# A 4 MB store of zero rows, issued behind the scan loop instead of ahead of it

## The reference

```python
h = rmsnorm(x) * (1 + sc1) + sh1
z = h @ w_in                                  # q | k | v | u
att = dilated_attn_prompt(q, k, v)            # or dilated_attn_decode with 2048 cached rows
ssm_y, hT_re, hT_im = s5_branch(u, h0, ...)   # scan over positions; last states are outputs
mixed = concat(rmsnorm(att), rmsnorm(ssm_y))
x = x + g1 * (mixed @ w_out)
h2 = rmsnorm(x) * (1 + sc2) + sh2
x = x + g2 * hier_moe(h2)                     # top 2 of 16 experts for each token
y = rmsnorm(x)
# outputs: y, new k and v, last scan states of the prompt (ssm_p) and of the samples (ssm_s)
```

## Time and profile before

| what | value |
|---|---|
| median of 3 runs | 1109.52 us (1108.87, 1109.52, 1143.79) |
| profiled execution, span from first to last instruction | 1138.1 us |
| mean granted TensorE clock in it | 0.855 |
| PE busy | 914.7 us (80%) |
| DVE busy | 378.3 us (33%) |
| POOL busy | 205.6 us (18%) |
| DMA moved | 231.09 MB, mean 203 GB/s |
| POOL's queue (q0) | 21.12 MB |
| the zero store | 4096 KB, issued at 369.99 us, landed 30.7 us later |

### The profile page before, as it was taken

The page is one execution under the profiler, slowest core; times in us unless marked ns, Lnnn a source line. Parts: engine busy times, 40 slices in busy tenths (PEclk is TensorE's granted clock), DMA queues, the critical chain, the costliest instruction groups (busy, mean ns, idle before and its releaser), DMA issues.

```text
span 1138.1 us, 11619 instructions
## 1 busy us (share of the span) xinstructions
PE 914.7 (80%) x4582; PEld 544.7 (48%) x4582; DVE 378.3 (33%) x790; ACT 162.5 (14%) x346; POOL 205.6 (18%) x311
## 2 busy tenths in 40 slices
PE   2525999999999665756769839999999999998920
PEld 2425884875666553543325434444444444444410
DVE  3021233112223989997126350111111111110118
ACT  1212000002224011011302100111111101111023
POOL 1234000014000466675100000000000000000043
PEclk9967999965569878778789758999999999999975
DMA  9969301160000936060343485498998999899252
GB/s 316 381 196 391 148 18 64 66 231 19 9 19 11 267 163 259 1 259 28 137 121 135 168 294 200 172 346 309 345 349 312 339 348 340 310 352 343 83 190 82
DMA packets 91428, 231.09 MB, mean 203 GB/s; under 512 B 3436, under 2 KB 12812, under 8 KB 89173
## 3 DMA queue, kind: packets, MB, share of 16 engines
q1 hardware_dynamic: 78630, 195.69, 47.8%
q0 software_dynamic: 5840, 21.12, 5.7%
q10 hardware_dynamic: 6912, 13.65, 3.2%
HBM read 213.37 MB, written 21.27 MB: 206 GB/s over the span
## 4 chain that ended last, share of the span: by engine, by line
PE 65%; DVE 14%; DMA 11%; issue 4%; SPq 4%; POOL 2%; ACT 1%; ACTq 0%; DVEq 0%; POOLq 0%
PE ps L1944 22%; PE ps L1963 11%; PE ps L1623 8%; DMA ring<-in_ada_w 5%; PE ps L1849 4%; PE ps L1532 4%; PE ps L1659 3%; PE ps L1657 3%; DMA out_ssm_s<-sample_states 3%; PE ps L1606 2%; PE ps L1675 2%; DVE s_xi L1169 2%; DMA ring<-in_w_in 2%; DVE s_gi L1182 2%; DVE s_gr L1180 2%
## 5 line engine op out<-in xcount | busy, mean ns | idle before, releaser
L1944 PE MATMUL ps<-ering,xgT 128*128 128x512 f32 x576 | 255.4, 597 | 5.0 <-ACT xgT L679 3.9
L1944 PEld LDWEIGHTS ps<-ering,xgT 128*128 128x128 f32 x576 | 108.8, 192 | 135.6 <-issue 133.3
L1963 PE MATMUL ps<-ering,aT 128*128 128x512 f32 x288 | 126.8, 593 | 3.1 <-ACT aT L679 3.1
L1623 PE MATMUL ps<-hT,ring 128*128 128x272 f32 x384 | 90.4, 399 | 1.9 <-DMA ring<-in_w_in 1.9
L1963 PEld LDWEIGHTS ps<-ering,aT 128*128 128x128 f32 x288 | 53.5, 190 | 64.8 <-issue 61.2
L1623 PEld LDWEIGHTS ps<-hT,ring 128*128 128x128 f32 x384 | 74.1, 193 | 17.9 <-issue 2.5
L645 POOL DMA_INDIRECT xg<-h_d,gidx x18 | 17.0, 943 | 338.8 <-PE ps L1532 305.0
L1849 PE MATMUL ps<-ring,mixT 128*128 128x512 f32 x128 | 63.5, 658 | 9.4 <-DVE pt L1314 9.1
L1543 PE MATMUL ps<-ring,silu_c 128*32 128x128 f32 x768 | 33.5, 347 | 43.3 <-DMA ring<-in_ada_w 42.6
L1453 DVE SCALAR_TENSOR_TENSOR a_s<-a_t,ps 128x512 f32<-128x512 f32 x18 | 12.4, 688 | 119.6 <-ACT a_t L679 119.6
L1543 PEld LDWEIGHTS ps<-ring,silu_c 128*32 128x32 f32 x768 | 29.6, 142 | 46.7 <-issue 32.5
(11 more groups left out here) (357 smaller groups left out, 1180.3 us busy)
## 6 DMA issues: line engine op xcount, KB each, us to landing
ering<-in_w_gate SPq DMA_DIRECT2D x18, 2048.0 KB, 14.6
ering<-in_w_up SPq DMA_DIRECT2D x18, 2048.0 KB, 20.2
ering<-in_w_down SPq DMA_DIRECT2D x18, 2048.0 KB, 9.8
ring<-in_ada_w SPq DMA_DIRECT2D x12, 2048.0 KB, 19.8
ring<-in_cache_k SPq DMA_DIRECT2D x8, 1792.0 KB, 9.9
ring<-in_cache_v SPq DMA_DIRECT2D x8, 1792.0 KB, 14.3
y_d<-ysb ACTq DMA_DIRECT2D x18, 512.0 KB, 8.2
ring<-in_w_in SPq DMA_DIRECT2D x4, 2048.0 KB, 18.3
```

What stands on the lines that cost most here:

```text
L1623: ins = mm(out, r[:, 512 * k + P * c:512 * k + P * (c + 1)], hT[:, k, cols], start=k == 0, stop=k == KD - 1)
L1944: ins = mm(ps[:, 2 * w + u, :], xgT[:, u, k, :], r[:, 512 * k:512 * (k + 1)], start=k == 0, stop=k == KD - 1)
L1963: ins = mm(ps[:, 6 + n, :], aT[:, u, c, :], r[:, D * c + 512 * n:D * c + 512 * (n + 1)], start=c == 0, stop=c == 3)
```

## The change

The line that issues the zero store is moved from its place ahead of the store of the samples' states to the place behind the 16 steps of the scan loop, ahead of the two stores of the prompt's last states. Nothing else is changed, in what is computed or in the waits.

```diff
         pool.dma_start(glu[:, 0, :, :], I["glu_a"]).then_inc(s("glul"), 16)
         pool.dma_start(glu[:, 1, :, :], I["glu_b"]).then_inc(s("glul"), 16)
 
-        pool.dma_start(y_d[NE * P:NTILE * P, :], I["zero"].partition_broadcast(EXTRA * P)).then_inc(s("yzero"), 16)
-
-
         pool.dma_start(O["ssm_s"], states[:, :]).then_inc(s("statest"), 16)
...
             pool.tensor_tensor(gi[b][:, :, :], gi[b][:, :, :], cs, ALU.mult).then_inc(s("hout"), 1)
+        pool.dma_start(y_d[NE * P:NTILE * P, :], I["zero"].partition_broadcast(EXTRA * P)).then_inc(s("yzero"), 16)
+
         pool.dma_start(O["ssm_p"][:, 0, :], las[:, :]).then_inc(s("ssmst"), 16)
         pool.dma_start(O["ssm_p"][:, 1, :], lai[:, :]).then_inc(s("ssmst"), 16)
```

## The result

The changed kernel takes a little longer. Its median is 1118.29 us (8 runs, 1113.13 to 1164.63), beside 1111.54 us before (8 runs, 1108.87 to 1160.11). Both sets hold executions with a lower granted clock that take some 3 to 5% longer, and the ratios in this document are formed without them. The ratio is 1.0056 with an interval of 1.0032 to 1.0080, that is 6.2 us (3.6 to 8.9). Both lie within the 2% band and on either side of the +3.7 us that was forecast.

What follows compares the result with a forecast made beforehand. It took the chain of waits as the bound, with DVE setting the loop's pace behind its 3.84 us wait. Terms -3.0 + 4.5 + 1.2 + 1.0 = +3.7 us, on a median of 1109.5, gave 1113 us; range 1105 to 1121.

Steps and rivals of the forecast that it cites:

- The wait at A: DVE, after step 2's scans, idles 3.84 us before the first decode instruction; removing this gains 3.0 us net.
- The loss: DVE's step 3 additions run beside POOL's last step 2 product: 0.8 us off the gain, bounds 0 and 1.0.
- The meeting with w_out: Output projection: zeros delay w_out's second half by 6.2 us; less 1.7 us of slack, PE loses 4.5 us.
- equal turns in time: Alternative price of the w_out meeting: the rest of w_out 4.7 us late, 3.0 us behind the slack.
- TensorE's clock behind the gap: Second half of the output projection's first 16 products: 1.2 us lost after PE's idling, bounds 0 and 2.5.
- The modulation loads: Loads behind the output projection's start meet the zeros' end for 1.5 us; cost 1.0 us, bounds 0 and 2.5.
- SP's wait for the prompt's states: The prompt's states' store lands behind the zeros on POOL's queue; 9 us of cover, so it costs nothing.
- the free meeting: Rival at w_out: zeros wait for it, slack and low DMA share hide the rest; -3.0 to -3.8 us, chance 0.25.
- Zeros first: Rival at L1849's second half: zeros take most engine time, price 19.4 us; +18.9 in all, 1128 us, chance 0.18.
- No gain: Rival: in a shorter execution zeros land before DVE asks, leaving only collisions; +6.7, 1116 us, chance 0.10.

Runs made afterwards that it cites:

- short_rows: The changed kernel with its 4 MB of zeros written in rows of 1 KB instead of 4 KB; ratio 1.0346 (1.0279 to 1.0413) to the kernel before.
- the second trace: The changed kernel itself, run and profiled again beside the variants; ratio 1.0026 (0.9996 to 1.0055) to the kernel before.
- wait_wout: The changed kernel, with POOL waiting for the second half of w_out to land before it issues the zero store; no ratio was measured.
- second_zero: The kernel before, zero store in its old place, plus a second 4 MB store of zeros behind the loop; ratio 1.0063 (0.9951 to 1.0175).
- half_end: Against the kernel before: 2 MB of zeros behind the samples' states' store, 2 MB at the end of the loop; ratio 1.0034 (1.0003 to 1.0065).
- step8_zero: Against the kernel before: zero store issued behind step 8 inside the scan loop; ratio 0.9989 (0.9957 to 1.0021).
- states_first: Against the kernel before: zero store at its old time, but behind the store of the samples' states; ratio 0.9972 (0.9890 to 1.0053).

## Why the prediction was right

*The wait at A.* Predicted: 3.84 us of idle time gone, 3.0 us net. Measured: the idle time is gone, and the net at step 4 is 2.6 us against the trace before, 1.4 against the second trace with the wait. The loss, put at 0.8 and at most 1.0, is 1.0 by the length of step 3 (8.3 us instead of 7.3), and the idle time itself is 3.84 us in one trace and 3.17 in the other. That this gain reaches the end of the loop nearly whole is borne out against the trace before only; against the second it is 0.4 to 0.5 us there, since the last step is set by PE too. The mechanism named for the loss, additions beside POOL's products, is what the traces show: 1.59 us beside POOL and 0.69 without, while the multiplications that read one input from PSUM keep their 0.68 us. The Trainium skill's page "GPSIMD Engine Reference", section "1. Specifications", says that GpSimd shares its SBUF interfaces with VectorE and that the two contend when a VectorE instruction has two SBUF inputs; these rows agree.

*The meeting with w_out.* Predicted 6.2 us of delay less 1.7 us of slack, 4.5 us on PE. Measured 5.0 and 5.2 us of delay (17.9 and 18.1 less 12.9) and a gap of 3.16 and 3.45 us. The place and the mechanism are right; the term was too large by a little over 1 us, and that it came so near is partly luck. It supposed zeros from 1.2 us behind their issue on, with 1.9 MB of w_out still to come; they came 4.2 us behind it, with 0.67 MB to come. And its 6.2 us came from another meeting and were held to be near equal turns in time; the turns are by packet, and a packet of zeros holds an engine about twice as long as one of w_out. By equal turns in time, 0.67 MB would have been 1.7 us late, no more than the slack: next to no gap. The two errors work against each other, and the figure of 4.7 us by equal turns fits the 5.0 for the same reason. The Trainium skill's page "DMA: Bandwidth & Descriptors", section "Queues, rings and completion order", says that a DMA engine goes round between the queues that have work, a packet at a time; the numbers of packets (131 and 135; 66 and 67 in short_rows) agree.

*TensorE's clock behind the gap.* Predicted 1.2 us, with 2.5 as the upper bound. Measured 1.6 us (5.17 less half of 7.13) and 3.1 us (6.66), and 2.4 with the second store (5.98). This term was too small, and 3.1 us lies beyond its bound: in the second trace nearly all of the eight products ran at the lower clock (0.50 from 568.5 to 572.5 us).

*The modulation loads.* Predicted 1.0 us; measured none, since the zeros were over in 24.9 us and SP's first issue came only then. The bound of 2.5 us above it held only in this order of events: wait_wout shows 7.7 us, and the argument that a DMA share of 0.39 leaves room was wrong.

*SP's wait for the prompt's states.* Predicted to be covered by 9 us. They landed at 550.96 + 24.0 = 575.0 us, SP came to the wait at 575.32 + 18.13 = 593.4: 18 us of cover.

*The sum.* +3.7 us, by -3.0 + 4.5 + 1.2 + 1.0. Measured by the traces from A to C: -2.61 + 5.28 = +2.7 us, and -2.69 + 6.39 = +3.7 in the second; by time 6.2 us (3.6 to 8.9) and 2.9 us (-0.4 to 6.1). That the second trace's sum is the forecast's is luck: the gap and the modulation loads were put too high, the clock too low. Of the rivals, the free meeting was excluded by the gap. Zeros first had its premise right, that engines which alternate by rows give the zeros most of the time, but its price of 19.4 us was far off, since little of w_out was left. No gain had its condition wrong, as second_zero's wait of 3.17 us shows, though the first timing (6.2 us) lies nearer to its +6.7 than to the forecast. Why it lies above the traces isn't settled. The traces of shorter executions hint at one reason: in them the gain is 0.4 to 0.5 us at the output projection, and half_end's B to C, with the gap of the change, is 6.6 us above step8_zero's, about +6 in all. These are single traces, and of neither the kernel before nor the changed one.

No version beat the kernel before by more than the measurement's uncertainty. Those with the states' store first and the zeros away from w_out and the modulation loads have the removal's gain in the traces, 0.4 to 3.0 us at the output projection, depending on the trace with the wait that they are held against (states_first's 4.5 has the last step's spread in it); in time no gain is shown.

## What to carry to other kernels

Price a late wait by the idle time of the engine that waits, not by the transfer's length in the chain: 31.86 us in the chain were 3.84 us of idle time and 1.4 to 2.6 us of gain a step later. When a large transfer is moved, look at each queue for the loads in flight at its new place and for when their consumers want them; a load with 1.7 us of slack did not stand the company of a transfer on another queue. To price such a meeting, count packets: what is left of the load when the other transfer begins to move, and how long one packet of the other holds an engine. A bulk transfer that nobody waits for is safer behind the critical loads on their own queue, where w_out lost nothing and the next loads 2.0 us, or in a stretch in which no load is awaited.

## What the runs showed of the hardware that was not expected

- Two queues with work moved as many packets as each other, whatever a packet's length: 131 and 135 in 2 us with packets of 159 and 84 ns, 66 and 67 in 4 us with packets of 845 and 115 ns.
- A transfer issued beside another that filled the engines moved nothing at first: the zeros for 4.2 us beside w_out, the modulation loads for over 4 us beside the zeros. With the engines free, the zeros' first packets moved within 1.0 us of the issue (at 369.99 us before). Why isn't settled.
- DRAM to DRAM, 4 MB of zeros landed 23.8 us after the issue in step8_zero and 24.9 in the change. Written in pieces of 1 KB they took 63.6 us, with the number of packets unchanged.
- The modulation loads' packets are small (1.47 MB in 2863 packets from 563 to 582 us before, some 512 B), and they lose far more beside such a store than their share of the engines suggests: 18.50 us of issues became 25.88 in wait_wout and 50.19 in short_rows.
